# Index scores and query-key products of two heads issued together on the two halves of the rows, in the second block's mixer

## The reference, cut to what matters

```python
def dsa_attention(pa, q_norm, k_norm):
    q, k, v, qi, ki, wi = split_cols(pa, ATT_SPLITS)      # 8 heads of 64, 2 key groups, 8 index heads of 64
    ...
    def block(args):                                      # 128 queries
        logits = jnp.einsum('bqhd,bsd->bqhs', qib, ki)    # the index scores, by head
        score = jnp.einsum('bqhs,bqh->bqs', jax.nn.relu(logits), wib)
        score = jnp.where(pos[None, None, :] <= tb[None, :, None], score, -jnp.inf)
        _, idx = lax.top_k(score, n_sel)                  # n_sel = 128
        ...
        s = jnp.einsum('bqgrd,bqkgd->bqgrk', qg, ks) * scale
        s = jnp.where(valid[:, :, None, None, :], s, -jnp.inf)
        p = jax.nn.softmax(s, axis=-1).astype(vs.dtype)
        o = jnp.einsum('bqgrk,bqkgd->bqgrd', p, vs)
```

## Time and profile before

| | us |
|---|---|
| median of 3 runs | 3794.18 |
| lowest and highest | 3789.75, 3802.14 |
| the profiled execution, its time | 3788.03 |
| its span, first to last instruction | 3786.2 |

### The profile page before, as it was taken

How to read it: one execution, slowest core, us unless ns; L and a number is a source line. 1 busy time by engine, 2 the same in 40 slices (tenths; PEclk the granted TensorE clock), 3 DMA queues, 4 the chain that set the end, 5 groups by cost and what they waited for, 6 DMA issues and landing times.

```text
span 3786.2 us, 55741 instructions
## 1 busy us (share of the span) xinstructions
PE 3639.9 (96%) x23104; PEld 3014.5 (80%) x23104; DVE 1969.6 (52%) x3453; ACT 1505.1 (40%) x2665; POOL 1620.2 (43%) x883
## 2 busy tenths in 40 slices
PE   9998999999899999999999899999999999889999
PEld 8877888878688878888767778888888866778887
DVE  2455554334645544553676635543652486755552
ACT  3343333434333343333555333334333455424332
POOL 3113666421166635663321135663665322214664
PEclk9999999999899999999999999999999999999999
DMA  4102332311143224322210034323332220012332
GB/s 127 40 29 90 111 102 70 88 45 40 51 132 104 76 86 141 101 67 88 72 40 2 3 101 131 103 66 115 100 100 84 81 57 17 3 35 89 100 100 95
DMA packets 393405, 291.95 MB, mean 77 GB/s; under 512 B 17056, under 2 KB 355904, under 8 KB 393152
## 3 DMA queue, kind: packets, MB, share of 16 engines
q1 hardware_dynamic: 387728, 284.49, 24.6%
q10 hardware_dynamic: 5136, 2.70, 0.4%
q0 software_dynamic: 288, 1.18, 0.1%
HBM read 286.24 MB, written 2.10 MB: 76 GB/s over the span
## 4 chain that ended last, share of the span: by engine, by line
PE 84%; DVE 8%; ACT 4%; POOL 2%; issue 1%; ACTq 0%; DMA 0%; POOLq 0%; DVEq 0%; SPq 0%
PE ps L802 13%; PE ps L803 13%; PE ps L804 13%; PE ps L1025 4%; PE ps L1026 4%; PE ps L1027 4%; PE ps L1577 3%; PE ps L928 3%; PE ps L931 3%; PE ps L930 3%; PE ps L1053 3%; PE ps L1071 2%; PE ps L1062 1%; PE ps L1133 1%; PE ps L829 1%
## 5 line engine op out<-in xcount | busy, mean ns | idle before, releaser
L3411 POOL TENSOR_TENSOR wl<-wraw,wh 128x1024 fp32r<-128x1024 f32 (+1 forms) x424 | 1027.3, 2428 | 1595.5 <-ACT wh L2742 1594.9
L802 PE MATMUL ps<-x_T,wh 128*128 128x512 f32 (+1 forms) x2224 | 849.8, 382 | 0.0
L803 PE MATMUL ps<-x_T,wh 128*128 128x512 f32 (+1 forms) x2224 | 848.3, 381 | 0.0
L804 PE MATMUL ps<-x_T,wl 128*128 128x512 f32 (+1 forms) x2224 | 848.3, 381 | 0.0
L2742 ACT ACTIVATE wh<-wraw 128x1024 fp32r<-128x1024 f32 (+1 forms) x424 | 445.9, 1053 | 778.6 <-PE ps L804 488.6
L802 PEld LDWEIGHTS ps<-x_T,wh 128*128 128x128 f32 x2224 | 418.2, 188 | 81.1 <-POOL wl L3411 0.7
L804 PEld LDWEIGHTS ps<-x_T,wl 128*128 128x128 f32 x2224 | 418.1, 188 | 81.0
L803 PEld LDWEIGHTS ps<-x_T,wh 128*128 128x128 f32 x2224 | 418.2, 188 | 80.0 <-issue 0.5
L2021 DVE TENSOR_TENSOR scr<-scr,ps 128x512 f32<-128x512 f32 x132 | 90.7, 687 | 464.9 <-ACT scr L2890 464.9
L1025 PE MATMUL ps<-wh,h_T 128*128 128x512 f32 x672 | 262.4, 390 | 0.2
L1027 PE MATMUL ps<-wh,h_T 128*128 128x512 f32 x672 | 261.5, 389 | 0.0
(11 more groups left out here) (779 smaller groups left out, 6920.1 us busy)
## 6 DMA issues: line engine op xcount, KB each, us to landing
wraw<-in_ffn_w_gate_dram SPq DMA_DIRECT2D x88, 512.0 KB, 3.9
wraw<-in_ffn_w_up_dram SPq DMA_DIRECT2D x88, 512.0 KB, 3.9
wraw<-in_w_in_dram SPq DMA_DIRECT2D x82, 512.0 KB, 3.7
wraw<-in_w_gate_dram SPq DMA_DIRECT2D x44, 512.0 KB, 3.8
wraw<-in_w_up_dram SPq DMA_DIRECT2D x44, 512.0 KB, 3.9
mix<-in_ffn_w_down_dram SPq DMA_DIRECT2D x20, 1024.0 KB, 6.8
arena<-in_ffn_w_down_dram SPq DMA_DIRECT2D x12, 1024.0 KB, 6.4
wraw<-in_ffn_w_down_dram SPq DMA_DIRECT2D x24, 512.0 KB, 3.6
```

What stands on the lines that cost most here:

```text
L802: mm(b[:, t0:t1], wh[:, k, :], xTh[:, k, t0:t1], k == 0, False)
L803: mm(b[:, t0:t1], wh[:, k, :], xTl[:, k, t0:t1], False, False)
L804: ins = mm(b[:, t0:t1], wl[:, k, :], xTh[:, k, t0:t1], False, k == 7)
L3411: tt(wl, raw_of(w), wh.bitcast(F32), ALU.subtract).then_inc(*g.sig("w", "lo", w))
```

## The change

`softmax` is split. For an even head `scores_of_two` takes two banks and issues the query-key products of this head and the next, alternating between the banks; the second bank is held. For the odd head `qk` is None: nothing is issued, and its bank is no longer held. Its later steps stay where they were. `index_sum` does the same with the index scores. Only PE's program changes.

```diff
+            def scores_of_two(l, u, qks, *ready):
+                us = [u[:1] + (u[1] + q,) + u[2:] for q in range(2)]
+                two = [bank(("qk", l, x), ("sm", "max" if masked(x) else "exp", l, x), hold=q == 1)
+                       for q, x in enumerate(us)]
+                for _, free in two:
+                    pe.wait_ge(*free)
+                for r in ready:
+                    pe.wait_ge(*at(*r))
+                last = len(qks[0]) - 1
+                for n in range(last + 1):
+                    for q, (b, _) in enumerate(two):
+                        c0, c1, lhs, rhs = qks[q][n]
+                        ins = mm(b[:, c0:c1], lhs, rhs, n == 0, n == last)
+                        if n == last:
+                            ins.then_inc(*pe.sig("sm", "qk", l, us[q]))
+
             def softmax(l, u, qk, vs, wide, *ready):
                 nk, nb = width(u), width(u) // P
+                if qk is None:
+                    held.discard(book.bank[("qk", l, u)])
+                elif isinstance(qk[0], list):
+                    scores_of_two(l, u, qk, *ready)
+                else:
+                    scores(l, u, qk, *ready)
+                yield
+                yield
+                yield from values_of(l, u, nk, nb, vs, wide)
...
-                qk = [(0, nk, qT[hb(h), h // 2, i * P:nk], kd[hb(h), g, 0:nk])]
-                if i == 0:
-                    qk.append((0, P, identr, cmaskr))
+                def qk_of(h):
+                    qk = [(0, nk, qT[hb(h), h // 2, i * P:nk], kd[hb(h), g, 0:nk])]
+                    return qk + ([(0, P, identr, cmaskr)] if i == 0 else [])
+
+                qk = None if h % 2 else [qk_of(h), qk_of(h + 1)]
...
             def index_sum(l, i, h):
+                if h % 2:
+                    held.discard(book.bank[("ix", l, i, h)])
+                    return
                 nk = (i + 1) * P
-                b, free = bank(("ix", l, i, h), ("pk", "relu", l, i, h))
-                pe.wait_ge(*free)
+                two = [bank(("ix", l, i, h + q), ("pk", "relu", l, i, h + q), hold=q == 1) for q in range(2)]
                 pe.wait_ge(*at("dsa", "iT", l, 3))
                 pe.wait_ge(*at("dsa", "kid", l))
-                mm(b[:, 0:nk], qiT[hb(h), h // 2, i * P:nk], kid[hb(h), 0:nk], True,
-                   True).then_inc(*pe.sig("pk", "ix", l, i, h))
+                for b, free in two:
+                    pe.wait_ge(*free)
+                for q, (b, _) in enumerate(two):
+                    mm(b[:, 0:nk], qiT[hb(q), h // 2, i * P:nk], kid[hb(q), 0:nk], True,
+                       True).then_inc(*pe.sig("pk", "ix", l, i, h + q))
```

More of the change, by code:

```diff
@@ L1044, in ffn, with scores @@
                                row=lambda k: ("ffn", "lo", n, k))
+            def scores_of_two(l, u, qks, *ready):
[13 more added lines that the diff above has]
+                            ins.then_inc(*pe.sig("sm", "qk", l, us[q]))
             def softmax(l, u, qk, vs, wide, *ready):
                 nk, nb = width(u), width(u) // P
+                if qk is None:
[7 more added lines that the diff above has]
+                yield from values_of(l, u, nk, nb, vs, wide)
+            def scores(l, u, qk, *ready):
                 b, free = bank(("qk", l, u), ("sm", "max" if masked(u) else "exp", l, u))
@@ L1054, in softmax, with values_of @@
                 ins.then_inc(*pe.sig("sm", "qk", l, u))
-                yield
-                yield
+            def values_of(l, u, nk, nb, vs, wide):
                 b, free = bank(("pt", l, u), ("sm", "ptc", l, u))
```

## The result

The changed kernel takes 3802.57 us in the median of 7 runs (3796.19 to 3804.87), the kernel before 3793.81 us in the 7 runs beside it. The medians are 8.8 us apart; the ratio is 1.0031, interval 1.0019 to 1.0043, which would be some 12 us. So it is slower, by 0.2 to 0.3%, just at the bound of 0.3% that the prediction set for telling it from no change. The forecast was 3798.6 us, 4.4 above before, in a range of 3783 to 3812.

The account below looks back on a forecast made before the run. PE looked the bound at 96% busy, but DVE was nearly full in query block 0 and new waits would end its rounds; 2 x (2.2 + 2.5) - 2.8 + 0.4 - 1.2 - 1.4 = +4.4 us, 3798.6 us, range 3783 to 3812.

Parts of the forecast that it names:

- The bank argument: Query block 0, seventh round: the index pair takes head 3's early-released bank and waits for its exp, starting at 1894.98.
- The wait: Query block 0: the index pair waiting for head 3's exp makes 13.80 us of 11.62, +2.2 us per layer.
- The clock: Behind PE's 3.9 us gap before the index pair: granted clock drops to 1.2 GHz, +2.5 us per layer, ends 0 and 3.3.
- the second cycle: Four rounds, DVE's column taps at 1887.81 to those at 1899.43: +2.2 us waiting and +2.5 us low clock per layer.
- the term for blocks 2 and 1: Query blocks 2 and 1: 2.2 us won, 2.0 given back before the last pair, 0.6 saved; taken as -0.7 per layer.
- Rival 3: Pairs do not overlap where heads differ in bank and weights, each product costing as a single: 3804 us, chance 0.03.
- Third and fourth cycle: Value products of heads 4 and 6 take heads 5 and 7's banks before their exp: +0.1 us each, +0.4 in all.
- query block 3: 512-column products before column taps: two pairs per layer gain 0.3 us each, -0.6 per layer, -1.2 in all.
- rival 2: Clock drops cost 3.3 us, another follows heads 6 and 7's wait, blocks 2 and 1 gain nothing before: 3811 us, chance 0.18.
- It is nearly full: DVE in query block 0: idle only 0.70 to 1.11 us before taps, 2.19 in layer 1, so little to give.
- Rival 1: PE is the bound in the mixer rounds and the saving arrives: 3759 us in full, 3777 with half; chance 0.09.
- The first cycle: Query block 0, rounds before the taps at 1887.81: shorter by 0.7 us in layer 0, 2.1 in layer 1, sum -2.8.

## Why the prediction was right, and where it was not

**The bank argument held, with its sizes.** The index pair was to start 0.15 us after head 3's exp: 0.14. Idle 3.9 us: 3.77. The wait 2.2 us: 2.0. The clock 2.5 us: 2.3 and 2.4. Holding that one bank takes all of it away. The Trainium skill (TensorE: Matmul & The Clock Gate, Why this matters for your kernels) wants gaps of TensorE short in mid-kernel; here the trace agrees at 3.77 us, in both layers. Shorter gaps went either way (last section).

**The total was in part luck.** The forecast had +4.4 us; the medians give +8.8, the ratio 12, and the profiled pair 13.6. It came out inside the range because the large term, the second cycle, was nearly right and the range was wide; the term for blocks 2 and 1 had the wrong sign.

**Pairs cost what one costs.** With banks held a pair of 384 columns takes 0.85 us to the next matmul (1885.88 to 1886.73), as one did. Rival 3 is out.

**Third and fourth cycle, query block 3.** +0.08 and -0.4 per layer, against +0.2 and -0.6. In block 3 the transposes of heads 2 and 3 of layer 0 started at 1944.55 and 1949.60, 5.05 us apart where it was 5.35: the 0.3 us of the forecast. The second still waits for ACT, 0.77 us.

**The step that failed is query blocks 2 and 1**, forecast at -0.7 per layer (its own terms, 2.2 - 2.0 + 0.6, give -0.8) and measured at +1.47 and +3.57. Its gross gain of 2.8 us came out nearer 2: with the banks held it is 2.0 us in layer 1 (59.17 against 61.15) and at least 1.9 in layer 0 (55.71, with 3.4 us of low clock in it, against the 57.61 at full clock); the 3.8 us against the profile before (59.46) are in part that profile's own low clock. Its losses were too small. I had listed only requests of the heads' products for a released bank and overlooked the one for head 5's transposes, with the warming products behind it: 1.8 us in layer 0. And I had given the last pair 2.0 us for its wait without the drop of clock behind it: 3.3 and 3.2. The 2.3 us that layer 1 lost beside (64.72 us against 62.38 with head 5's bank held) have the 10.2 us at 0.50 in them that no new wait stands in front of; their cause stays open. The drop behind the last pair was in rival 2, so a part of what rival 2 describes came true; its price of 17 us did not.

**One reason was put too strongly.** "It is nearly full" of DVE was read as if DVE ended the cycles. The lighter DVE shows that PE did. The sentence mattered little for the forecast, since the new wait ended the cycles of the changed kernel, but it made me expect less of a mended version: a second cycle of 10.9 to 11.3 us where 10.43 came. The Trainium skill (TensorEngine Tiling (Array Packing), PSUM Bottleneck) says that the copying out of PSUM may become the bound once TensorE is packed. After the mend another engine is the bound, by 0.4 us a cycle (9.89 against 9.47), DVE being without a gap; but what was made lighter to show it were its top-k steps, which read no PSUM, so this is near to what the Trainium skill states and does not show it.

**Rival 1** was out as forecast, and not for want of PE as a bound: of the 35.1 us, 12 arrive as soon as no bank is given away early. The rest runs into DVE in block 0 and into maximum, exp and transposes in blocks 3, 2 and 1; for the latter I have the rows, no run.

## What to carry to other kernels

When a rotation hands out buffers, a buffer is free when its reader is done and not when its writer has issued its last instruction; list everything that asks for a buffer behind an early release, fillers included, and see whose reader it then waits for. Before a saving is counted off a nearly full engine, make the next engine lighter for one run: it tells in the cycle length which of the two is the bound. A change that loses may hold a gain under it: here holding the bank of the odd head turned +0.3% into -0.3%.

## What was not expected of the hardware

- The length of a gap alone did not tell whether the clock fell. Behind 2.36 us of idle time in block 2 of the changed kernel, with nine warming products ahead, it stayed at 1.00; behind the same wait in the kernel before, 2.14 us with the same nine ahead, it was at 0.50 for 6.6 us. Changed kernel, layer 0:

```profile
1993.75 0.55 PE L1090 MATMUL ps<-cr,scr 128*128 128x128 f32 x3 [2.36 <-ACT scr L3174]
...
1993.70:1998.00 4.30, 4.25 (x20) 2.53 (x21) 4.07 (x15) 2.19 (x8) 2.86 (x3) 1.00 0.00 0
```

- So it went with other gaps of about 2 us: at 1.00 behind 1.83 us with eleven products ahead, at 0.50 behind 1.91. There the eight products took 2.93 us where with the banks held they start at once and take 1.67, with 1.24 us of idle time behind them, and the clock stays up:

```profile
1987.85 1.67 PE L754 MATMUL ps<-cr 128*128 128x384 f32 x8
1990.75 0.44 PE L1090 MATMUL ps<-cr,scr 128*128 128x128 f32 x2 [1.24 <-ACT scr L3176]
```

- Stretches at 0.50 come and go in executions of kernels that are alike at the place. Here are the same 3.4 us in front of the first cycle in the changed kernel and in the one with the hold in block 0. PE is busy throughout both, 1.5 us behind a wait of 2.66 us for POOL that both have:

```profile
1865.30:1868.70 3.40, 3.40 (x16) 2.82 (x15) 2.63 (x5) 3.36 (x7) 0.23 (x1) 1.00 0.44 129
```

```profile
1863.70:1867.10 3.40, 3.40 (x9) 2.65 (x8) 2.66 (x5) 3.36 (x7) 0.21 (x1) 0.51 0.46 138
```

The low one costs 1.6 us: the next column's taps come 7.56 us after those before them in the first (1869.01 to 1876.57) and 9.16 in the second (1867.42 to 1876.58). The first cycle has such a difference too. Before, it had a clock of 1.00 in layer 0 (11.59 us) and of 0.90 in layer 1 (13.09); after, of 0.86 in both (11.37 and 11.34). At a full clock a first cycle with pairs takes 10.81 us (layer 0 with head 5's bank held, layer 1 with all held). So the pairs are worth 0.8 us there, as forecast for layer 0; the 2.1 us that layer 1 was to give, and the 1.75 that it gave, belong to cycles with low clock in them. Two profiles are best compared stretch by stretch, with the clock of each, and the 2.4 us of the span that I couldn't place may be no more than this; no run settles it.
